# Moving the activation pair x_hi, x_lo by 64 bytes in SBUF

## What is computed

```python
x = layer_norm(DEEPNORM_ALPHA * x + mixer(x), ln_g[i], ln_b[i])      # mixer: even layer, then odd layer
x = x + ((p[i] @ w_pl[i]) * sigmoid(x @ w_pl_gate[i]))
...
h = h + swa_mixer(rms_norm_2(h, attn_norm), w_qkv, sinks, w_o)
h = h + relu(rms_norm_2(h, mlp_norm) @ w_up)**2 @ w_down
return rms_norm_2(h, final_norm)
```

## Time and profile before

| | us |
|---|---|
| median of 3 executions | 957.06 (952.76 to 957.85) |
| profiled execution | 950.61 |
| its span, first to last instruction | 948.8 |
| PE busy in it | 914.2 |
| mean granted clock of PE | 0.996 |

### The profile page before, as it was taken

How to read it: one execution, slowest core, us unless ns; L and a number is a source line. 1 busy time by engine, 2 the same in 40 slices (tenths; PEclk the granted TensorE clock), 3 DMA queues, 4 the chain that set the end, 5 groups by cost and what they waited for, 6 DMA issues and landing times.

```text
span 948.8 us, 19419 instructions
## 1 busy us (share of the span) xinstructions
PE 914.2 (96%) x7694; PEld 840.0 (89%) x7694; DVE 467.2 (49%) x967; ACT 499.2 (53%) x702; POOL 673.8 (71%) x486
## 2 busy tenths in 40 slices
PE   5999899999999999999999999999998999999997
PEld 5899899998998889999999999788896789998886
DVE  3448854469453252666676666616637352221004
ACT  3675433573235465555666556556557346554341
POOL 3787655557555797967666677668797549989983
PEclk9999999999999999999999999999999999999999
DMA  5769357556443565745444544465573237766641
GB/s 178 207 209 170 102 145 116 137 127 113 134 126 120 189 198 161 216 137 148 144 130 137 156 141 150 136 204 162 154 229 91 79 101 221 214 189 208 203 133 45
DMA packets 131251, 146.12 MB, mean 154 GB/s; under 512 B 11022, under 2 KB 95960, under 8 KB 131160
## 3 DMA queue, kind: packets, MB, share of 16 engines
q1 hardware_dynamic: 129176, 140.64, 52.1%
q10 hardware_dynamic: 1984, 4.24, 1.3%
HBM read 143.81 MB, written 1.05 MB: 153 GB/s over the span
## 4 chain that ended last, share of the span: by engine, by line
PE 76%; DVE 8%; POOL 5%; issue 4%; ACT 3%; DMA 2%; SPq 1%; DVEq 0%; ACTq 0%; POOLq 0%
PE dense L555 21%; PE dense L557 20%; PE dense L556 20%; DMA raw<-in_w_in_even_dram 2%; POOL wlo L530 2%; PE bank L930 2%; POOL wlo L529 2%; POOL lg L515 1%; PE bank L825 1%; DVE cv L1761 1%; PE bank L821 1%; ACT whi L1175 1%; PE bank L840 1%; PE dense L624 1%; PE bank L987 1%
## 5 line engine op out<-in xcount | busy, mean ns | idle before, releaser
L530 POOL TENSOR_TENSOR wlo<-raw,whi 128x512 fp32r<-128x512 f32 (+1 forms) x263 | 411.3, 1570 | 25.4 <-ACT whi L1175 25.3
L529 POOL TENSOR_TENSOR wlo<-raw,whi 128x512 fp32r<-128x512 f32 x199 | 258.2, 1297 | 214.2 <-ACT whi L1175 213.9
L1175 ACT ACTIVATE whi<-raw 128x1024 fp32r<-128x1024 f32 x264 | 276.0, 1058 | 251.0 <-PE dense L557 199.8
L555 PE MATMUL dense<-x_hi,whi 128*128 128x256 f32 x1232 | 355.2, 288 | 10.3 <-POOL wlo L524 5.8
L556 PE MATMUL dense<-x_lo,whi 128*128 128x256 f32 x1232 | 342.9, 278 | 0.0
L557 PE MATMUL dense<-x_hi,wlo 128*128 128x256 f32 x1232 | 342.8, 278 | 0.0
L555 PEld LDWEIGHTS dense<-x_hi,whi 128*128 128x128 f32 x1232 | 232.3, 189 | 18.0 <-issue 9.0
L556 PEld LDWEIGHTS dense<-x_lo,whi 128*128 128x128 f32 x1232 | 232.6, 189 | 1.8 <-issue 1.7
L557 PEld LDWEIGHTS dense<-x_hi,wlo 128*128 128x128 f32 x1232 | 232.6, 189 | 0.0
L555 PE MATMUL dense<-whi,ya_hi 128*128 128x512 f32 x192 | 78.0, 406 | 0.7 <-issue 0.7
L557 PE MATMUL dense<-whi,ya_lo 128*128 128x512 f32 x192 | 75.0, 391 | 0.0
(11 more groups left out here) (331 smaller groups left out, 1404.1 us busy)
## 6 DMA issues: line engine op xcount, KB each, us to landing
raw<-in_w_in_odd_dram SPq DMA_DIRECT2D x64, 512.0 KB, 3.8
raw<-in_w_in_even_dram SPq DMA_DIRECT2D x32, 512.0 KB, 7.7
raw<-in_w_in_even_dram SPq DMA_DIRECT2D x64, 256.0 KB, 4.6
raw<-in_mlp_w_up_dram SPq DMA_DIRECT2D x32, 512.0 KB, 4.2
raw<-in_mlp_w_down_dram SPq DMA_DIRECT2D x32, 512.0 KB, 4.5
raw<-in_w_out_even_dram SPq DMA_DIRECT2D x16, 512.0 KB, 3.8
raw<-in_w_pl_gate_dram SPq DMA_DIRECT2D x16, 512.0 KB, 4.6
raw<-in_w_out_odd_dram SPq DMA_DIRECT2D x16, 512.0 KB, 3.9
```

What stands on the lines that cost most here:

```text
L529: pool.tensor_tensor(wlo[:, slot, 0:half], unit_slot(u)[:, 0:half], whi[:, slot, 0:half].bitcast(F32), ALU.subtract)
L530: pool.tensor_tensor(wlo[:, slot, first:2 * half], unit_slot(u)[:, first:2 * half], whi[:, slot, first:2 * half].bitcast(F32), ALU.subtrac ...
L555: pe.matmul(out_, lh, rh, start=start, stop=False, skip_group_check=True)
L1175: act.activation(whi[:, u % NSPL, :], unit_slot(u), ACT.Copy).then_inc(hi_done, 1)
```

## The change

`x_hi`, `x_lo` and `rsum` move 64 bytes down, to place 0 modulo 256; the second filler grows by the same 64 bytes, so that `xtok` and everything behind it keep their addresses. No instruction is added, removed or reordered, and no shape or wait changes. `rsum`, 32 bytes of reciprocals for the attention, is written by DVE and read by POOL (L515). The offset becomes 128 both with x moving and with x stationary.

```diff
-        ctx.enter_context(nc.sbuf_tensor("quarter_ahead", [P, (192 - used) % 256 // 4], F32))
+        ctx.enter_context(nc.sbuf_tensor("half_ahead", [P, (128 - used) % 256 // 4], F32))
         x_hi = sb("x_hi", [P, KT, T], F32R)
         x_lo = sb("x_lo", [P, KT, T], F32R)
         rsum = sb("rsum", [P, 2, 4])
-        ctx.enter_context(nc.sbuf_tensor("in_step", [P, 8], F32))
+        ctx.enter_context(nc.sbuf_tensor("in_step", [P, 24], F32))
         xtok = sb("xtok", [P, NT, D])
```

## The result

| | before | after |
|---|---|---|
| median of 5 executions each | 956.57 us | 963.99 us (962.49 to 965.04) |
| profiled execution | 950.61 us | 962.65 us |
| its span | 948.8 us | 960.9 us |

The ratio is 1.0083, with a 95% interval of 1.0061 to 1.0106: slower by 0.8%. The profiles are 12.0 us apart, the medians 7.4.

The account below looks back on a forecast made before the run. The prediction took PE's matmul steps as the bound: 730 more slow x steps at 4.45 ns give +3.2 us, all else nothing, so 957.1 + 3.2 = 960.3 us. The range was 949.5 to 972 us.

Parts of the forecast that it names:

- slow throughout: Rival: every x matmul step, `up` included, takes the slow value; +10.6 us, 967.6 us; chance 0.27.
- What bounds the kernel: PE, busy 914.2 of 948.8 us, sets the time; a matmul's cost goes almost one to one into it.
- losses count in full: Slower x steps on PE, and faster ones too, were to reach the end of the kernel undiminished.
- Two values of the step: x matmuls on PE step at 113.3 ns (free) or 117.8 ns (slow), and keep it for the run.
- Nothing from rsum, and from the writes of x: Moving rsum and the ACT and DVE writes of x was costed at nothing.
- The slow share between the neighbours: Of 3,899 x steps, 0.58 slow at offset 128, between 0.35 and 0.80: 730 more, +3.2 us; chance 0.36.
- 128-byte period: Rival: offset 128 acts as offset 0, every x step costs 120.0 ns; +19.3 us, 976.4 us; chance 0.07.
- free throughout: Rival: no x step is slow, offset 128 being farthest from offset 0; -6.8 us, 950.3 us; chance 0.22.
- no effect: Rival: place doesn't matter, timing alone makes the two states of x steps; no change, 957.1 us; chance 0.08.
- Carrying the profile over to the median: The +3.2 us was added to the median of 957.1 as to the profiled 950.6, keeping their 6.4 us difference.

## Why the prediction was right or wrong

The time, 963.99 us, lies in the range (949.5 to 972.0), and it moved the way the forecast did. But the forecast was +3.2 us and the measured change is +7.4 between medians and +12.0 between profiles, and the outcome that I held likeliest, within 0.5%, isn't the one that came; slower by more had 0.35. That the sign came out is in part luck: it rests on a mean of two shares that the runs refute, and the range held the measured time because it reached up to the rival "slow throughout".

- **What bounds the kernel.** Right in the main: most of the loss of the x steps went into the span, 14.1 us of loss against 12.0 us of span. Over seven profiles, span less loss is 941.7 (before), 941.5 (before, moved as a whole), 940.0 (x at 192), 939.7 (after), 941.5 (after, moved as a whole), 941.4 (x at 128) and 945.3 us (x at 240). The last four hold 1.6, 2.7, 2.6 and 2.6 us of x steps at the 1.2 GHz level; without them they are 938.1, 938.8, 938.8 and 942.7. So the rest of the span is some 3 us shorter where the loss is 21 us or more, that is, slower steps save some waiting elsewhere, and "losses count in full" was a little too much.
- **Two values of the step.** Right for offsets 64 and 192 with both parts of x at one place: once settled, long runs step at 113.3 or 117.8, and a run keeps its value.
- **Nothing from rsum, and from the writes of x.** Right to within 0.1 us: DVE's three groups that write x_lo take 692, 708 and 691 ns for one, all three 691 before; the 708 is four instructions.
- **The slow share between the neighbours.** This is the step that failed. I took the mean of two shares, 0.35 and 0.80, and the price of 4.45 ns from them. Offset 128 has no free state at all and two values of its own, 118.7 for most runs and 120.0 for some. At 118.7 - 113.3 = 5.4 ns for every step, 3,899 x 5.4 = 21 us; the profile has 21.2, where the sum had 10.0 (2,250 x 4.45). The places are not a scale on which one can interpolate: the full table jumps by up to 8 ns from one multiple of 4 bytes to the next. A small slip beside it: the 3,537 steps with x moving count 24 whose partner is a tile of 16 columns, free before and after; the 3 x 1232 have 3,513 steps under 130 ns, which changes the sum by 0.1 us.
- **The rival "slow throughout"** had the right shape, all runs and `up` with them, at +10.6 us; the price was at least 1 ns too low per step. Its reason, that the streams meet late in the weight load, isn't shown by any run. The rival of a 128-byte period fell (offset 0 costs 120.0 and offset 128 118.7), and so did "free throughout", which took distance from the worst offset for safety.
- **The rival "no effect"** fell. It would have left 957.1, and with ACT and POOL still, the same matmul steps at 113.3, 118.7 or 120.0 ns by place alone. The Trainium skill's page SBUF — State Buffer, section "Who interferes with whom", gives TensorE two independent read ports and says that it never waits on anyone. Where the places of its own two operands are concerned, these steps speak against a reading of that rule by which place can't matter, and the measurement decides.
- **Carrying the profile over to the median.** This failed too, and hid part of the first error. I added the change to the median as if the profiled execution of before stood for the others. It doesn't: at 950.61 us it is below all 49 other executions of that kernel (the lowest took 952.76), its loss is 7.1 us, and the same offsets elsewhere gave 10.6. The kernel after lost 21.2 us, and 20.9 moved as a whole, so its profile (962.65) is near its median (963.99). I had put the spread of 5 us down to the starts of runs. They may be one part. The time also goes with PE's mean granted clock: of 44 executions of the kernel before for which it is listed, four at 0.997 took 953.9 us on the mean and four at 0.990 took 959.4. At an equal clock of 0.995, before takes 955.6 (11 executions) and after 964.9 (two): 9 us, between the two differences above. These executions come from more than one chip.

Still open: what makes the two streams lock. The runs show that the offset of the places matters, that an offset can have two values of which a run takes one near its start, and that a run locks as a whole. What picks the value isn't shown: behind idle, offset 64 took 117.8 in two kernels of matmuls alone and 113.3 in the third. Where in a matmul the streams meet, and what is shared, no run shows.

## What to carry to other kernels

Where PE is the bound, read the start-to-start steps of its matmuls, not their durations: where the same instruction at the same clock has two steady values, as here 113.3 and 117.8 ns, something else than the work sets the step. Time the candidate placements with a kernel of matmuls alone, one run per place and several kinds of start, before moving anything; one profile of 580 us ranked the four offsets in the order of loss that the whole kernel then had (7.1 to 10.6, 15.5, 21.2 and 24.9 us), though the times of the last two don't tell them apart. Don't interpolate between places, and place for the shape at hand: of the four places 64 bytes apart, 256 columns ran worst at the weights' place and 512 columns best.

## What was not expected of the hardware

- Place alone moves the step of a 128x128 by 256-column float32r matmul between 113.3 and 123.3 ns at full clock, in steps of 4 bytes: 240 gives 113.3, its neighbours 236 and 244 give 120.0 and 121.6.
- Many of the steady means are simple ratios of 6.67 ns, the time of 16 cycles at 2.4 GHz: 113.3 = 17 x 6.67, 117.8 = 53/3 x 6.67, 118.7 = 89/5 x 6.67, 120.0 = 18 x 6.67, and with 512 columns 226.7 = 34 and 233.3 = 35. The last steps of an offset-128 run at the lower value repeat with a period of five matmuls, 5 x 118.67 = 89 x 6.67. This reads like two periodic processes locked to each other; it is a pattern in the numbers and not a cause that was shown.
- Mixed places of x_hi and x_lo are no compromise: twelve mixed pairs, five starts each, and none free (116.9 to 121.3 ns).
